# Softmax scores as three fp32r products of split queries and keys, with the split on ScalarE and GpSimd and the first decay totals on GpSimd

## The reference

```python
h = rms_norm(x, mix_norm_g)
proj = h @ w_in                      # 4096 columns: da_q, da_k, da_v, hg_q, hg_zf, hg_zb, hg_i, hg_g
# group A, 4 heads: two softmaxes of half-heads of width 64
q = apply_rope(rms_norm(q, q_g)) * 64 ** -0.5 ;  k = apply_rope(rms_norm(k, k_g))
scores = einsum('bhcqd,bhckd->bhcqk', q, k)       # c = 0, 1: the two halves
weights = softmax(scores)[:, :, 0] - lam * softmax(scores)[:, :, 1]
o = weights @ v ; y_a = rms_norm(o, out_g) * (1 - lam_init)
# group B, 4 heads: gated linear recurrence, forward and backward, state 128 x 128
y_b = rms_norm(scan(q, k_f, v, log_f) + flip(scan(flip ...)), out_g) * silu(gate)
x = x + concat(y_a, y_b) @ w_out
x = x + conv_glu_ffn(rms_norm(x))                 # 1024 -> 2 x 2816 -> conv of width 3 -> gate -> 1024
```

## Time and profile before

| | us |
|---|---|
| median of 3 runs | 1360.7 (1360.37 to 1361.06) |
| the profiled execution's own time | 1361.43 |
| its span, first to last instruction | 1359.6 |
| PE busy in the span | 1339.1 (98%) |
| DVE busy | 911.3 (67%) |
| POOL busy | 659.5 (49%) |
| ACT busy | 641.9 (47%) |

### The profile page before, as it was taken

One profiled execution on the slowest core, in us unless ns is written; L12 is line 12 of the kernel. 1 busy time (PEld: TensorE's weight loads), 2 busy tenths in 40 slices (PEclk: granted clock), 3 DMA queues, 4 the chain that ended last, 5 costly groups with the idle time before them and its releaser, 6 DMA issues.

```text
span 1359.6 us, 20826 instructions
## 1 busy us (share of the span) xinstructions
PE 1339.1 (98%) x7970; PEld 1084.7 (80%) x7970; DVE 911.3 (67%) x1058; ACT 641.9 (47%) x948; POOL 659.5 (49%) x475
## 2 busy tenths in 40 slices
PE   9999999999999999999999999999999999999999
PEld 6778777777888888888877787778788888888887
DVE  7787897665888888600358968975658888885001
ACT  7354667574444444321443546666644444443121
POOL 2553575247444444444565536752564444444443
PEclk9999999999999999999999999999999999999999
DMA  5322222122323333332323222121233323322333
GB/s 188 94 85 80 63 63 71 47 78 85 101 93 99 103 94 93 99 106 93 93 93 93 80 74 68 55 73 45 79 103 98 93 94 103 99 93 93 99 102 109
DMA packets 37140, 121.43 MB, mean 89 GB/s; under 512 B 5056, under 2 KB 5440, under 8 KB 37056
## 3 DMA queue, kind: packets, MB, share of 16 engines
q1 hardware_dynamic: 36768, 119.75, 28.5%
q10 hardware_dynamic: 288, 0.52, 0.1%
HBM read 113.96 MB, written 2.10 MB: 85 GB/s over the span
## 4 chain that ended last, share of the span: by engine, by line
PE 80%; DVE 9%; ACT 4%; issue 4%; POOL 2%; DMA 0%; ACTq 0%; DVEq 0%; POOLq 0%
PE bank L584 24%; PE bank L586 24%; PE bank L585 24%; PE bank L731 2%; DVE QQ L1467 2%; POOL wL L520 1%; PE bank L674 1%; PE bank L749 1%; DVE hL L422 1%; ACT wH L916 1%; PE bank L703 1%; PE bank L740 1%; POOL rstd L434 1%; DVE sqR L1387 1%; PE bank L619 1%
## 5 line engine op out<-in xcount | busy, mean ns | idle before, releaser
L520 POOL TENSOR_TENSOR wL<-raw,wH 128x1024 fp32r<-128x1024 f32 x142 | 343.2, 2417 | 404.3 <-ACT wH L916 294.1
L584 PE MATMUL bank<-hH,wH 128*128 128x512 f32 x1216 | 484.0, 398 | 2.0 <-DVE hL L422 1.8
L586 PE MATMUL bank<-hL,wH 128*128 128x512 f32 x1216 | 474.7, 390 | 0.0
L585 PE MATMUL bank<-hH,wL 128*128 128x512 f32 x1216 | 474.1, 390 | 0.0
L584 PEld LDWEIGHTS bank<-hH,wH 128*128 128x128 f32 x1216 | 228.6, 188 | 66.1 <-issue 14.5
L514 POOL TENSOR_TENSOR wL<-raw,wH 128x256 fp32r<-128x256 f32 x204 | 184.2, 933 | 190.2 <-ACT wH L916 190.2
L586 PEld LDWEIGHTS bank<-hL,wH 128*128 128x128 f32 x1216 | 228.5, 188 | 48.9
L585 PEld LDWEIGHTS bank<-hH,wL 128*128 128x128 f32 x1216 | 228.9, 188 | 45.4 <-issue 0.5
L916 ACT ACTIVATE wH<-raw 128x1024 fp32r<-128x1024 f32 x173 | 182.6, 1056 | 146.4 <-PE bank L586 146.3
L1626 DVE TENSOR_TENSOR x<-x,bank 128x512 f32<-128x512 f32 x16 | 10.9, 682 | 200.7 <-PE bank L586 200.7
L584 PE MATMUL bank<-gH,wH 128*128 (+1 forms) x352 | 137.2, 390 | 0.0
(11 more groups left out here) (172 smaller groups left out, 1730.2 us busy)
## 6 DMA issues: line engine op xcount, KB each, us to landing
raw<-wts SPq DMA_DIRECT2D x210, 512.0 KB, 3.5
x<-xT SPq DMA_DIRECT2D x8, 256.0 KB, 5.7
swp<-K SPq DMA_DIRECT2D x32, 64.0 KB, 2.0
swp<-QO SPq DMA_DIRECT2D x32, 64.0 KB, 2.4
outT<-x SPq DMA_DIRECT2D x8, 256.0 KB, 2.0
raw<-wts ACTq DMA_DIRECT2D x2, 256.0 KB, 4.8
raw<-wts SPq DMA_DIRECT2D x2, 256.0 KB, 5.9
W<-pos SPq DMA_DIRECT2D x1, 256.0 KB, 5.9
```

The lines of the kernel that those rows point to most:

```text
L520: pool.tensor_tensor(wL[:, s, :], raw[:, s, :], wH[:, s, :].bitcast(F32), ALU.subtract)\
L584: pe.matmul(out, wH[:, s, a:a + P], rhs_h, start=first, stop=False)
L585: pe.matmul(out, wL[:, s, a:a + P], rhs_h, start=False, stop=False)
L586: return pe.matmul(out, wH[:, s, a:a + P], rhs_l, start=False, stop=last)
```

## The change

PE's scores read fp32r halves of queries and keys: a high part rounded by ACT (`rope_split`) and a low part by POOL (`rope_rest`, the float32 tile minus its high part, in place). Each step has three products (high x high, low x high, high x low) of 512 columns for each c, six matmuls, accumulated in the same two banks; c alternates within each product. The first step of each head waits for the semaphore `qk_low` of POOL in place of `scaled` of DVE. The high parts lie in storage of the recurrence that is free by then.

ACT and POOL do their part of a head's keys or queries in the slot after `rope`'s (slots 15, 16, 18, 23, 24, 27, 28), ACT ahead of `assemble` and the item's copies, POOL after its split of the next weight unit. The queries of head 1, needed in slot 21, are done in slot 20 itself (`URGENT`), on ACT after the exponentials and on POOL as the last thing of the slot.

The first totals (L1476) leave DVE's `grow` and go to POOL, after its split, in slots 8 and 20.

```diff
+URGENT = 20
...
+                    def rope_rest(n):
+                        kind, hd = ROPES[n]
+                        pool.wait_ge(*qk_high.at(l, n + 1))
+                        pool.tensor_tensor(rope_low(kind, hd), rope_tile(kind, hd), rope_high(kind, hd).bitcast(F32), ALU.subtract)\
+                            .then_inc(qk_low.sem, 1)
+
+                    def first_totals(pair):
+                        pool.wait_ge(*hg_k.at(l, 7 * pair + 1))
+                        pool.wait_ge(*hg_q.at(l, 9 * pair + 3))
+                        for d in range(2):
+                            w = totals(pair, 1)[:, d, :].rearrange("p (n two) -> p n two", two=2)
+                            nxt = pool.tensor_tensor(totals(pair, 2)[:, d, :], w[:, :, 0], w[:, :, 1], ALU.mult)
+                        nxt.then_inc(tot_ready.sem, 1)
...
@@ POOL's slot, after split(s + 1)
+                        if n is not None and n % PAIR_ITEMS == 1:
+                            first_totals(n // PAIR_ITEMS)
+                        if s == URGENT:
+                            rope_rest(ROPES.index(STATS[s - 1]))
+                        if STATS.get(s - 2) in ROPES and s - 1 != URGENT:
+                            rope_rest(ROPES.index(STATS[s - 2]))
...
@@ PE, scores(a)
                         if qt == 0:
-                            pe.wait_ge(*scaled.at(l, JOB[("dq", hd)] + 1))
+                            pe.wait_ge(*qk_low.at(l, 2 * hd + 2))
-                        for c in range(2):
-                            r = slice(HD * c, HD * c + HD)
-                            m = pe.matmul(bank[4 + c][:], QO[r, hd, qt * P:qt * P + P], K2[r, hd % 2, :],
-                                          start=True, stop=True)
+                        for n, (q, k) in enumerate(((qH, kH), (qL, kH), (qH, kL))):
+                            for c in range(2):
+                                r = slice(HD * c, HD * c + HD)
+                                m = pe.matmul(bank[4 + c][:], q[r, at], k[r, :], start=n == 0, stop=n == 2)
...
@@ ACT
+                    def rope_split(n):
+                        kind, hd = ROPES[n]
+                        act.wait_ge(*scaled.at(l, JOB[ROPES[n]] + 1))
+                        if hd in (1, 2):
+                            act.wait_ge(*kt_mm.at(l, 4))
+                        elif hd:
+                            act.wait_ge(*av_mm.at(l, 2))
+                        act.activation(rope_high(kind, hd), rope_tile(kind, hd), ACT.Copy).then_inc(qk_high.sem, 1)
...
@@ ACT's slot, after the squares and ahead of gate, tokens, assemble and item
+                        if STATS.get(s - 2) in ROPES and s - 1 != URGENT:
+                            rope_split(ROPES.index(STATS[s - 2]))
...
@@ ACT's slot, after the exponentials
+                        if s == URGENT:
+                            rope_split(ROPES.index(STATS[s - 1]))
...
@@ DVE, evict
                         elif kind == "dq":
                             dst = rope_tile(kind, hd)
+                            if hd >= 2:
+                                dve.wait_ge(*sc_mm.at(l, 4))
...
@@ DVE, grow
-                        if lv == 1:
-                            dve.wait_ge(*hg_q.at(l, 9 * pair + 3))
-                            dve.wait_ge(*hg_k.at(l, 7 * pair + 1))
-                            for d in range(2):
-                                w = totals(pair, 1)[:, d, :].rearrange("p (n two) -> p n two", two=2)
-                                nxt = dve.tensor_tensor(totals(pair, 2)[:, d, :], w[:, :, 0], w[:, :, 1], ALU.mult)
-                            nxt.then_inc(tot_ready.sem, 1)
```

More of the change, by code:

```diff
@@ L174, in build @@
     mix = ExitStack()
+    rounded = ExitStack()
     heads = ExitStack()
@@ L234, in build @@
         mix.close()
+        KR = sb("KR", [P, 2, HEADS * S], F32R, rounded)
+        sb("KR_QR", [P, 2 * HEADS * S], F32, rounded)
+        QR = sb("QR", [P, 2, HEADS * S], F32R, rounded)
+        sb("QR_OR", [P, 4 * HEADS * S], F32, rounded)
+        OR = sb("OR", [P, HEADS, S], F32R, rounded)
+        K2R = sb("K2R", [P, 2, S], F32R, rounded)
+        rounded.close()
         yH = sb("yH", [P, KT, S], F32R, heads)
@@ L295, in build @@
         oh_ready = signal("oh_ready", 4)
+        qk_high = signal("qk_high", 2 * HEADS)
+        qk_low = signal("qk_low", 2 * HEADS)
         sc_mm = signal("sc_mm", STEPS)
@@ L408, in rope_tile, with rope_high, rope_low @@
             return K2[:, hd % 2, :] if kind == "dk" else QO[:, hd, :]
+        def rope_high(kind, hd):
+            first = 0 if kind == "dk" else 1
+            if hd == 0:
+                return OR[:, 2 + first, :]
+            if hd == HEADS - 1:
+                return QR[:, 1, first * S:(first + 1) * S]
+            return KR[:, hd - 1, first * S:(first + 1) * S]
+        def rope_low(kind, hd):
+            return K2R[:, hd % 2, :] if kind == "dk" else OR[:, hd, :]
         def out_head(kind, hd):
@@ L725, in scores @@
                         if qt == 0:
-                            pe.wait_ge(*scaled.at(l, JOB[("dq", hd)] + 1))
+                            pe.wait_ge(*qk_low.at(l, 2 * hd + 2))
                         if a:
                             pe.wait_ge(*exps.at(l, a))
-                        for c in range(2):
-                            r = slice(HD * c, HD * c + HD)
-                            m = pe.matmul(bank[4 + c][:], QO[r, hd, qt * P:qt * P + P], K2[r, hd % 2, :],
-                                          start=True, stop=True)
+                        qH, qL = rope_high("dq", hd), rope_low("dq", hd)
+                        kH, kL = rope_high("dk", hd), rope_low("dk", hd)
+                        at = slice(qt * P, qt * P + P)
+                        for n, (q, k) in enumerate(((qH, kH), (qL, kH), (qH, kL))):
+                            for c in range(2):
+                                r = slice(HD * c, HD * c + HD)
+                                m = pe.matmul(bank[4 + c][:], q[r, at], k[r, :], start=n == 0, stop=n == 2)
                         m.then_inc(sc_mm.sem, 1)
```

## The result

The changed kernel takes 1371.88 us, the median of 4 runs (1371.61 to 1372.68); beside it the kernel before took 1360.86 us, the median of 4. The ratio is 1.0081, with a 95% interval of 1.0069 to 1.0093. It is slower by 11.0 us; I had predicted 3.8, and a range that ended at 1371.0. The profiled execution spans 1370.1 us, 10.5 more than before.

The account below looks back on a forecast made before the run. PE, busy 1339.1 of 1359.6 us, was taken as the bound. Layer 0 +1.4, layer 1 +1.7 and clock +0.7 made +3.8 us: 1365.2 from the profiled 1361.4, or 1364.5 against the median; range 1357.5 to 1371.

Parts of the forecast that it names:

- the three places I named: PE's waits grow in slot 10 (+1.4 us a layer), slot 15 (+0.9 and +1.2) and slots 20 to 24 (+1.2 a layer).
- The step: PE's score step: three fp32r pairs take 0.89 us instead of 1.06, gaining 0.18 with unrounded starts, 5.8 over 32 steps.
- showing loads: Rival: weight loads show in the row halves, a step takes 1.1 us with no gain, 1369 us in all; chance 14%.
- serial halves: Rival: a step's row halves don't overlap in fp32r, 22 us worse than forecast, 1380 and more; chance 4%.
- ACT's part: Slot 15: the rounding copy ahead of `A` makes PE wait longer, +0.9 us in layer 0 and +1.2 in layer 1.
- First totals in slot 8: Totals take about 2.0 us on POOL against 1.30 on DVE, delaying slot 10's item on PE: +1.4 us a layer.
- Slots 20 to 24: POOL's totals and subtraction delay head 1's first step by 1.8 us; after catching up, net +1.2 us a layer.
- POOL's part: Subtractions in slots 15 to 18 and 23 to 28 cost zero, up to 0.5 us a layer in slots 23 and 24.
- The clock: Longer wait in slot 21 likelier drops PE to half clock in both layers: 1.2 us in layer 0 at even odds, +0.7.
- other-side rival: The gain comes through: PE's waits stay as long, only the 5.8 us less slot 15's copy count, 1355 to 1356.5; chance 15%.

Follow-up runs that it names:

- single-edit runs: First totals put back on DVE in the changed kernel, 1369.95 us; only the first totals moved to POOL in the kernel before, 1362.5 us.
- products alone: Kernel before with three fp32r products a step, all reading the same rounded tile written by DVE, no ACT or POOL work, totals on DVE: 1360.04 us.

## Why the prediction was wrong in size

The direction and the three places I named were right. The sum was 3.8 and the trace says 10.5. By its own steps:

**The step** was right: 0.89 predicted, 0.89 to 0.91 measured. The rivals of showing loads (1.1 us a step) and of serial halves (1.58) fall. "TensorE: Matmul & The Clock Gate" of the Trainium skill, section Part 3, lets loads overlap only where row groups differ; here loads of a half that is at work stay hidden, as the rows of PEld and the 0.23 us between the second and third pair show, and the measurement decides. From start to start only 0.14 a step arrives, 4.5 us instead of 5.8. I have not traced the missing 0.02 to 0.04 a step.

**ACT's part**: slot 15 was predicted at +0.9 and +1.2 and measured at +0.80 and +1.17. The run with a late copy shows that the cause is the one given.

**First totals in slot 8**: predicted +1.4 a layer, measured +1.05. The totals took the 2.0 us I gave them. The penalty of 0.4 for L541 being overlapped was 1.2, but I had nothing for the 1.0 us that L547 wins back. Both single-edit runs show the term by itself.

**Slots 20 to 24**: the wait grew by 1.87 and 1.85, as predicted (1.8), but by another route, so the match is luck. I let `rope` begin at 154.6 and end at 158.4, with POOL's totals behind it; it began at 155.52, and the totals ran into it and doubled its last two operations. The net was +1.2 in the prediction and is +1.4 and +1.6, without slot 24's wait and half clock. I took 0.4 off for `W` in both layers, but the earlier trace rows list one such wait, in layer 0; there it is gone under the half clock, and in layer 1 PE didn't wait for `W` in slot 21 before. The four short steps brought 0.15 each, and the wait for `ev` in slot 23 fell by 0.2 in layer 0 and grew by 0.3 in layer 1.

**POOL's part is the step that failed.** "In slots 15 to 18 and 23 to 28 it ends before its first step on PE ... Zero, up to 0.5 a layer in slots 23 and 24, where it would slow DVE's two-input work." I asked who waits for the subtraction, and nobody does. The question was what it blocks. In slot 23 it takes 1.1 us from DVE, whose `ev` PE waits for in slot 24 as it does in slot 23: 1.2 us a layer. I had slot 23's row for that wait, and the row for the mutual blocking, and used neither here. The run with this subtraction a slot later shows cause and size, and that it only moves the loss; the run of the products alone, without it, has slot 24 as before. "Slot 27" was costed at nothing too and lost 0.8 and 1.2 us. There the subtraction isn't the cause of most of it: the run of the products alone has no subtraction and lost 0.65 in each layer, with the order of POOL's split and DVE's `rope` turned; and the run with float32 steps from slot 21 to 28 lost nothing. That the faster step turned the order is read from the starts (DVE first by 0.07 before, POOL first by 0.09 there); no run moved one of the two alone. The remaining 0.5 of layer 1 is a second such meeting, in slot 26. Together, both slots are 4.4 us of the 6.7 that were missing.

**The clock** was predicted at +0.7, and is +2.9: behind slot 21 in layer 0 (0.8), slot 24 in layer 0 (1.6) and slot 10 in layer 1 (0.5). I had named slots 21, 10 and 15 and put even odds on one. The mistake is the number of falls and not the price: the three new ones cost 1.0 each on average, against my 1.2, and the executions above show 0.6 to 1.3. What decides whether the clock falls isn't settled, and no run took the falls away alone: where they went, a wait went too. Counted from start to start, behind slot 21's 3.9 us it fell in all ten cases (five kernels, two layers); behind 2.0 to 2.5 us there, in one layer of two in each of four kernels; behind 2.8, in both; behind 1.7 and 1.9, in none of four; behind the same 2.54 us in slot 10, in six of eight; behind 2.24 in slot 24, in three of twelve.

The rest of the 6.7 is small: +0.9 for the steps outside slots 20 to 24, +0.6 for those slots, -0.8 for slots 10 and 15, and -0.6 from the start of the execution, which differs in every trace (0.05 to 0.6 us earlier than in that of before) and isn't the change's.

**The other-side rival**, that the gain comes through, failed for a reason which the products alone show: even with no work on ACT or POOL, 1.3 of 4.5 us arrive, since PE's next wait in slot 21 is set by DVE and takes what was won ahead of it (0.5 a layer), and slot 27 takes 0.65 more.

## What to carry to other kernels

Work put on an idle GpSimd is not priced by who waits for it, but by what VectorE does at that time: here a subtraction of 1.7 us that nobody waited for cost VectorE 1.1 and the kernel 1.0. A gain ahead of a wait that another engine sets is no gain; shorten that wait first (here by doing `rope` ahead of the totals, -1.9 us, of which 1.3 at equal clock), then apply the cheaper product only where its new chain isn't the last to arrive (heads 0 and 3, -3.6 us in all). And where two engines start operations within 0.1 us of each other that hold each other up, a faster third engine may turn their order: here VectorE lost 0.5 us by it, and TensorE 0.65.

## What the runs showed of the hardware

- Six fp32r products on two row halves take 0.90 us in either program order. Issued half by half they still run in pairs.
- A VectorE multiply of 128x512 with two SBUF inputs takes 0.69 us alone and 1.2 to 1.4 beside GpSimd's split or multiply; two of them beside its subtraction take 2.38 together, 1.28 without it, and the GpSimd subtraction takes 1.27 alone and 1.72 to 1.75 beside VectorE (both directions in the timelines above); in slot 27 DVE was held up where POOL had started first, by 0.09 or 0.10 us, and not where DVE had, by 0.07. "SBUF — State Buffer" of the Trainium skill, section Who interferes with whom, states such a lock, and these rows agree.
- A fall to half clock cost 0.5 to 1.6 us, by the starts of PE's items in two traces, and 0.6 to 1.3 by the executions of two kernels (the kernel before, and all heads split with `rope` first). The shortest waits ahead of one were 2.0 us from start to start (the kernel before, slot 21) and 2.24 (slot 24).
